# Products of the identity into unread PSUM, ahead of and behind the tiles of the input norm and ahead of the last masks of the routing

## The reference, cut to what matters

```
h = layer_norm(x, ln_in_g, ln_in_b)                       # the input norm
for l in range(2):
    q, k, v, u = split_projection(h, w_in[l])
    a = diff_attention(q, k, v, ...)                      # 4 heads, two softmax maps each
    p = pool_mixer(u, ...)                                # trailing means of 2/4/8/16 rows
    h = layer_norm(ALPHA * h + concat(a, p) @ w_out[l], ln1)
    probs = softmax(h @ router_w)                         # the routing: one of 4 groups,
    e_idx, gate = group_then_top2(probs + router_b)       # then 2 of its 4 experts
    h = layer_norm(ALPHA * h + sum(gate * expert(h)), ln2)   # 16 SwiGLU experts, 1024 -> 512 -> 1024
```

## Time and profile before

| | us |
|---|---|
| median of 3 runs (982.03 to 986.46) | 982.48 |
| the profiled execution | 983.06 |
| its span, first to last instruction | 981.3 |
| PE busy | 943.9 |
| PE weight loads busy | 785.0 |
| DVE busy | 822.3 |
| ACT busy | 657.7 |
| POOL busy | 260.4 |
| mean granted TensorE clock | 0.985 |

### The profile page before, as it was taken

The page is one execution under the profiler, slowest core; times in us unless marked ns, Lnnn a source line. Parts: engine busy times, 40 slices in busy tenths (PEclk is TensorE's granted clock), DMA queues, the critical chain, the costliest instruction groups (busy, mean ns, idle before and its releaser), DMA issues. The chain is left out here.

```text
span 981.3 us, 15260 instructions
## 1 busy us (share of the span) xinstructions
PE 943.9 (96%) x5118; PEld 785.0 (80%) x5118; DVE 822.3 (84%) x1211; ACT 657.7 (67%) x941; POOL 260.4 (27%) x343
## 2 busy tenths in 40 slices
PE   4999999999999999999989999999999999999994
PEld 4998867688888888888779988787888888888883
DVE  7977667789989899899866676588999898998997
ACT  4446541378888888888745566317788888888882
POOL 1433343471111111110323333425211111111012
PEclk8999999999999999999989999999999999999998
DMA  9863850599999999998894033529999999999965
GB/s 353 281 174 121 266 190 38 189 366 407 379 363 367 364 366 367 374 374 323 234 298 158 27 133 136 190 82 348 411 401 373 369 367 369 367 366 375 331 196 151
DMA packets 85550, 278.28 MB, mean 284 GB/s; under 512 B 8771, under 2 KB 11067, under 8 KB 85470
## 3 DMA queue, kind: packets, MB, share of 16 engines
q1 hardware_dynamic: 66880, 240.40, 66.9%
q0 software_dynamic: 11040, 21.14, 7.5%
q10 hardware_dynamic: 7566, 15.96, 4.7%
HBM read 266.51 MB, written 30.37 MB: 303 GB/s over the span
## 5 line engine op out<-in xcount | busy, mean ns | idle before, releaser
L1565 DVE TENSOR_TENSOR w_lo<-ring,w_hi 128x1024 fp32r<-128x1024 f32 x256 | 303.1, 1235 | 36.0 <-ACT w_hi L2200 33.6
L2200 ACT ACTIVATE w_hi<-ring 128x1024 fp32r<-128x1024 f32 x256 | 261.4, 1060 | 39.6 <-PE PS L1094 26.6
L1046 PE MATMUL PS<-w_hi,x_hi 128*128 128x512 f32 x512 | 163.9, 401 | 0.0
L1051 PE MATMUL PS<-w_lo,x_hi 128*128 128x512 f32 x512 | 160.7, 395 | 0.0
L1046 PE MATMUL PS<-w_hi,x_lo 128*128 128x512 f32 x512 | 160.0, 394 | 0.0
L1572 DVE TENSOR_TENSOR w_lo<-ring,w_hi 128x1024 fp32r<-128x1024 f32 x128 | 153.6, 1220 | 4.4 <-ACT w_hi L2213 4.4
L2213 ACT ACTIVATE w_hi<-ring 128x1024 fp32r<-128x1024 f32 x128 | 135.6, 1061 | 29.6 <-PE PS L1051 27.9
L2565 POOL DMA_INDIRECT M<-xs,idx x30 | 56.2, 1874 | 235.4 <-PE PS L1025 204.0
L1046 PEld LDWEIGHTS PS<-w_hi,x_lo 128*128 128x128 f32 x512 | 96.3, 188 | 23.2
L1051 PEld LDWEIGHTS PS<-w_lo,x_hi 128*128 128x128 f32 x512 | 96.5, 188 | 22.1
L1046 PEld LDWEIGHTS PS<-w_hi,x_hi 128*128 128x128 f32 x512 | 94.0, 189 | 19.6
(11 more groups left out here) (292 smaller groups left out, 1609.7 us busy)
## 6 DMA issues: line engine op xcount, KB each, us to landing
ring<-in_w_gate SPq DMA_DIRECT2D x32, 2048.0 KB, 14.4
ring<-in_w_down SPq DMA_DIRECT2D x32, 2048.0 KB, 14.8
ring<-in_w_up SPq DMA_DIRECT2D x32, 2048.0 KB, 15.6
ring<-in_w_in SPq DMA_DIRECT2D x8, 2048.0 KB, 16.8
ring<-in_w_out SPq DMA_DIRECT2D x4, 2048.0 KB, 8.8
ys<-H SPq DMA_DIRECT2D x2, 3072.0 KB, 20.0
H<-ys POOLq DMA_DIRECT2D x12, 512.0 KB, 8.4
M<-in_cache_k ACTq DMA_DIRECT2D x8, 512.0 KB, 3.7
```

The source lines that it names most:

```text
L1046: pe.matmul(PS[:, n, :], x[:, c:c + P], w_hi[j][:, k * 512:(k + 1) * 512], start=(j == 0 and k == 0 and x is x_hi[par]), stop=False)
L1051: mm = pe.matmul(PS[:, n, :], x_hi[par][:, c:c + P], lo[:, k * 512:(k + 1) * 512], start=False, stop=(j == 3 and k == 1))
L1565: dve.tensor_tensor(lo, w, w_hi[j][:, :].bitcast(F32), ALU.subtract).then_inc(up_lo, 1)
L2200: act.activation(w_hi[j][:, :], quarter(3 * par + n, j)[0], ACT.Copy).then_inc(up_hi, 1)
```

## The change

TensorE's program gets a helper that multiplies the identity by itself, 128 x 128 by 128 x 128 in float32, into a part of PSUM that nothing reads. It is called `count` times 9, 3, 8 and 6 ahead of the four tiles of the input norm, 3 times behind them, and 3 times in `rank` for the last tile of each layer, behind the wait for the exponentials and the ranks before and ahead of the wait for the masks. No wait is added or removed, and no other engine's program changes.

```
+            def keep_busy(count, bank, at):
+
+                for _ in range(count):
+                    pe.matmul(PS[:, bank, at:at + P], ident, ident, start=True, stop=True, skip_group_check=True)
+
...
                 pe.wait_ge(ex_done, 4 * l + n + 1)
                 if n >= 1:
                     pe.wait_ge(rank_read, 4 * l + n)
+                if n + 1 == len(tiles):
+                    keep_busy(3, bank, 2 * P)
                 pe.wait_ge(mask_done, 4 * l + n)
...
             pe.wait_ge(early_in, 16)
             for n in range(4):
+                keep_busy((9, 3, 8, 6)[n], 7, 0)
                 turn_z(n)
+            keep_busy(3, 7, 0)
```

## The result

The change is slower: 989.68 us against 983.94 us (medians of 8 runs each; 987.29 to 992.61 and 982.03 to 988.89), a ratio of 1.0051 with an interval of 1.0036 to 1.0067. By the ratio that is 5.0 us (the medians lie 5.7 apart) where 1.2 were forecast, and the time is outside the range. One execution of e4_more_code, of 12, took 1568.54 us at a granted clock of 0.556; it is in the median of 986.19 and not in the ratio.

A forecast was written before the change was run, and what follows sets the result against it. The experts were taken as bound by TensorE, so time ahead of them counts where its chain is latest. Norm 0, layer 0 routing +0.5, layer 1 +0.75 made +1.25 us; on the 982.48 median, 983.7 us, range 980.3 to 986.2.

The forecast's parts named there:

- rival 3: Input norm: the clock stays low and 29 products at 0.41 us delay TensorE; up to +4.4 us there, 988.1; chance 0.13.
- signs of being wrong: A clock of 1.00 from 196 to 205 us, or the first 400-column matmul of L698 later than 25.5.
- The longer wait in the first projection: At L698, TensorE's gain of 0.7 to 1.3 us becomes a wait of 1.7 to 2.3 us; value 0.
- The nine products: Ahead of the input norm's first tile: 3.7 us at 0.41 each, 4.84 to 8.5, making nothing late.
- The start is at the low level: Up to about 12.5 us the clock was read as low, despite the profile's 1.00; products there priced at 0.41 us.
- DVE's chain decides: Input norm: a faster TensorE gets none of DVE's work ahead of the fourth tile's `FThi` done sooner; value 0.
- rival 1: Layer 0's three routing products keep the clock up at 200.2 us; -0.45 us, 982.0; chance 0.22.
- Layer 0's routing: Three products, 0.75 us, less a 0.24 us wait ahead of L662: +0.5 us; lower end +0.15.
- The fall near 200: Layer 0, first expert: the 3.4 us low clock at 200.2 us stays; without it 1.7 us would be won.
- Layer 1's routing: Three products without cover, since TensorE is already late for L662: +0.75 us.
- Rival 2: Behind layer 0, the half-microsecond shift moves clock falls: 980.0 if some go (0.08), 985.4 if one comes (0.07).

The follow-up runs named there:

- e4_more_code: The change plus 16 products of 16 x 16 by 16 columns at the very start, 64 more instructions; 986.19 us, 1.0012 against the kernel before.
- e3_small_products: The change with every added product cut to 16 x 16 by 16 columns, same number of instructions; 988.92 us, 1.0041 against the kernel before.
- e1_norm_only: The change with only the input norm's 29 products, without the 3 in each routing; 989.08 us, 1.0039 against the kernel before.
- e7_change_again: The change run once more, unaltered, for a second profile; one run, 990.72 us.
- e2_rank_only: The change with only the 3 products in each routing, without the input norm's; 986.62 us, 1.0011 against the kernel before.
- e5_between_layers: The kernel before plus eight products ahead of the turn of the rows between the layers; 984.14 us, 1.0014 against the kernel before.
- e8_before_again: The kernel before run once more, unaltered, for a second profile; one run, 984.69 us.
- e9_code_34: The kernel before plus 34 products of 16 x 16 by 16 columns at the very start, 136 instructions; 988.27 us, 1.0033 against the kernel before.
- e10_code_24: The kernel before plus 24 products of 16 x 16 by 16 columns at the very start, 96 instructions; 985.73 us, 1.0018 against the kernel before.

## Why the prediction was wrong

- **The failed step: the added instructions were priced as work alone.** The sum counted products at 0.25 us each, less the wait that covers them. That 32 of them, 128 instructions, stand ahead of the turn between the layers had no term, and this is where 3.5 to 4 of the 5 us are (e3_small_products with no work: 1.0041; e4_more_code with more instructions: 1.0012). No rival held it either; rival 3, slower for the low clock in the norm, had the right sign for a wrong reason. None of the signs of being wrong came (the 400 columns started at 25.23, not behind 25.5, and the clock fell at 202.5): all of them lay at places that the added work touches, and the loss lay elsewhere.
- **The longer wait in the first projection: seen, and its consequence left out.** I wrote that TensorE's gain in the norm ends in a wait of 1.7 to 2.3 us at L698, value 0. The wait is 2.3 us, as worked out. But behind it the clock fell at 25.0 us, where TensorE is the latest: eight matmuls of 400 columns took 3.00 us instead of 1.70, and 1.4 us were lost. It happened in two of the four profiles that have the norm's full products and that wait unfilled (at 25.0 and, in e4_more_code, at 26.4 us; not in e1_norm_only and e7_change_again), so an estimate of the term is some 0.7 us on average (half of 1.4) and not 0. The eight other profiles have no fall there; that fits a fall brought by the wait, and doesn't show it.
- **What was right in the norm.** The nine products took 3.91 us of weight loads, 3.7 forecast. The start is at the low level, against the printed 1.00: the first eight transposes still take 1.97 us and the second eight 1.04. DVE's chain decides: the 400 columns start at 25.23, 0.42 later, as much as DVE's first normalised tile is late (8.42 against 7.99), ahead of any work of TensorE on it. The clock was up from the second tile to 25.0 us, and the norm won nothing by it.
- **What the products did to the clock.** The wish behind the change came true. In the five profiles with the full products the second eight transposes take 1.04 to 1.09 us; in the seven without them 1.63 to 1.97, and in five of these (e2_rank_only, e5_between_layers, e8_before_again, e9_code_34, e10_code_24) the low level lasts until 20.4 to 22.4 us, under a printed 1.00. Yet the 400 columns start at 24.50 to 25.23 us with them and at 24.70 to 24.93 without. This bears on rival 1 too: its reading that float32 transposes alone brought the level up at 12.5 is that of one execution; in e2_rank_only, e5_between_layers and e8_before_again the same transposes did not.
- **Layer 0's routing.** Forecast +0.5 us for L662. Measured: L669 (L662 before) starts 1.45 us after the first of the last keys instead of 1.09, +0.36; three products take 0.76 us, 0.25 each as priced. The fall near 200 stayed (202.5), as taken.
- **Layer 1's routing.** Forecast +0.75 with nothing to hide it. L666 is 0.67 us later, near the forecast, and then at 681.9 the shift is 0.8 us smaller: TensorE waits 0.64 us there for the gathered rows in the kernel before, a wait that was not among my rows, and most of the delay went into it. In this profile the term is about 0.
- **Rival 2, falls moving with the shift**, was right in kind (a new one at 154.7, the one at 500 gone from 504), but it needs no shift: e8_before_again has falls at new places without any change.
- **Spread.** The 3 runs shown reached from 982.0 to 986.5; 29 runs of the same kernel reach from 982.5 to 991.1. The base itself, 982.48, was 1.5 us under the median of 8 runs, 983.94.

The lines of the changed kernel behind the points on the norm and on layer 0's routing:

```profile
5.20 3.91 PEld L598 LDWEIGHTS PS<-CT 128*128 128x128 f32 x18 [5.20 <-DMA CT<-in_table]
...
9.28 1.97 PE L610 MATMUL PS<-CT,N 128*128 128x128 f32 x8
...
11.87 1.04 PE L610 MATMUL PS<-CT,N 128*128 128x128 f32 x8
...
25.23 3.00 PE L705 MATMUL PS<-FThi,wp_hi 128*128 128x400 f32 x8 [2.31 <-ACT FThi L1985]
...
197.27 0.60 PE L996 MATMUL PS<-CT,QK 128*128 128x128 f32 x4
197.71 0.83 PE L598 MATMUL PS<-CT 128*128 128x128 f32 x6
198.47 0.32 PE L666 MATMUL PS<-N,CT 128*16 128x16 f32 x6
198.72 0.21 PE L669 MATMUL PS<-N,CT 16*16 16x16 f32 x2
```

Still open: how much of the difference between e4_more_code (1.0012) and before is the clock's and how much the routing's, since both are inside the intervals; what the falls follow, in their moment; and why the second instruction load starts only some 6 us after the first.

## What to carry to other kernels

Count the instructions that a change puts ahead of a branch, not only their work. In this kernel, where TensorE runs dense short instructions right behind a taken branch, the place of the edge cost 4 us, and 64 harmless instructions more at another place gave it back. Look for `issue` as the releaser of a long wait in the middle of a group that has no wait in the code, and set it beside the instruction loads of the trace. Filling waits to keep the clock up did what it was to do in the norm, and no filled wait of this case made the time shorter clear of the noise: where another chain decides, as in the norm, the gain becomes a longer wait, and in two of four profiles a fall of the clock came behind that.

## What was not expected of the hardware

- A stand of TensorE of 2.2 to 4.6 us whose place follows the number of instructions ahead of it exactly (sum 154 in four programs), and that 64 further instructions remove. It ends 2.3 to 2.6 us after the start of a 16 KB instruction load, in all six profiles that have it.
- The printed granted clock of 1.00 ahead of the first recorded step is not a measurement: eight transposes of one shape took 1.97 us under it at 9.28 us and 1.04 us at 11.87.
- The low stretches, of 3.4, 6.8 or 10.2 us, change in number and place between executions of one program.
